# Gate and up projections: the order of rounded-weight and residue matmuls, two contraction tiles at a time

## What is computed

```python
def swiglu(h, w_gate, w_up, w_down):
    return (jax.nn.silu(h @ w_gate) * (h @ w_up)) @ w_down

x = x + swiglu(rms_norm(x, ffn_norm[i]), w_gate[i], w_up[i], w_down[i])
```

## Time and profile before

| | before |
|---|---|
| median of 3 runs | 1276.21 us (1276.15 to 1276.36) |
| span of the profiled execution | 1274.6 us |
| instructions | 17805 |
| matmuls | 7056, and as many weight loads |
| granted TensorE clock, mean | 0.999 |
| DMA, mean over the span | 176 GB/s |

### The profile page before, as it was taken

How to read it: one execution, slowest core, us unless ns; L and a number is a source line. 1 busy time by engine, 2 the same in 40 slices (tenths; PEclk the granted TensorE clock), 3 DMA queues, 4 the chain that set the end, 5 groups by cost and what they waited for, 6 DMA issues and landing times.

```text
span 1274.6 us, 17805 instructions
## 1 busy us (share of the span) xinstructions
PE 1263.7 (99%) x7056; PEld 1088.4 (85%) x7056; DVE 904.9 (71%) x1283; ACT 717.6 (56%) x1059; POOL 104.9 (8%) x137
## 2 busy tenths in 40 slices
PE   9999999999999999999999999999999999999997
PEld 8998778888888888888888888888888998888886
DVE  6967665776676685776666857777667897766665
ACT  5865454655555684654445545555555865654543
POOL 2000000000000440000000000000000781000000
PEclk9999999999999999999999999999999999999999
DMA  8443236465663312355554643686654523455551
GB/s 293 166 165 133 99 103 225 139 230 212 223 229 123 138 65 102 133 203 193 199 198 165 211 162 132 237 300 226 213 212 170 193 111 132 170 203 203 193 177 62
DMA packets 32802, 224.42 MB, mean 176 GB/s; under 512 B 3776, under 2 KB 4160, under 8 KB 7248
## 3 DMA queue, kind: packets, MB, share of 16 engines
q1 hardware_dynamic: 32576, 223.22, 49.3%
q10 hardware_dynamic: 144, 0.07, 0.0%
HBM read 222.23 MB, written 1.05 MB: 175 GB/s over the span
## 4 chain that ended last, share of the span: by engine, by line
PE 98%; DVE 1%; DMA 0%; ACT 0%; issue 0%; POOL 0%; ACTq 0%; SPq 0%; DVEq 0%; POOLq 0%
PE pb L496 25%; PE pb L467 16%; PE pb L469 16%; PE pb L468 16%; PE pb L498 13%; PE pb L473 3%; PE pb L1049 2%; PE pb L563 1%; PE pb L860 1%; PE pb L884 1%; PE pb L565 1%; PE pb L624 1%; PE pb L636 1%; PE pb L1108 0%; DMA xt<-d_x 0%; PE pb L691 0%
## 5 line engine op out<-in xcount | busy, mean ns | idle before, releaser
L1678 DVE TENSOR_TENSOR wlo<-raw,whi 128x2048 fp32r<-128x2048 f32 (+2 forms) x194 | 428.0, 2207 | 188.1 <-ACT whi L1162 187.7
L496 PE MATMUL pb<-both,whi 128*128 128x512 f32 x1344 | 476.0, 398 | 0.0
L1162 ACT ACTIVATE whi<-raw 128x2048 fp32r<-128x2048 f32 (+1 forms) x196 | 372.0, 1900 | 66.1 <-PE pb L469 59.6
L498 PE MATMUL pb<-both,wlo 128*128 128x256 f32 x1344 | 377.2, 281 | 0.0
L496 PEld LDWEIGHTS pb<-both,whi 128*128 128x128 f32 x1344 | 252.4, 188 | 61.5
L467 PE MATMUL pb<-whi,both 128*128 128x512 f32 (+2 forms) x728 | 286.3, 393 | 0.0
L469 PE MATMUL pb<-whi,both 128*128 128x512 f32 (+2 forms) x728 | 282.0, 387 | 0.0
L468 PE MATMUL pb<-wlo,both 128*128 128x512 f32 (+2 forms) x728 | 281.4, 386 | 0.0
L498 PEld LDWEIGHTS pb<-both,wlo 128*128 128x128 f32 x1344 | 253.8, 189 | 1.5
L1165 ACT ACTIVATE arena<-pb 128x256 f32<-128x256 f32 (+1 forms) x234 | 94.9, 418 | 243.4 <-PE pb L498 159.6
L469 PEld LDWEIGHTS pb<-whi,both 128*128 128x128 f32 x728 | 136.6, 188 | 28.8
(11 more groups left out here) (159 smaller groups left out, 1192.5 us busy)
## 6 DMA issues: line engine op xcount, KB each, us to landing
raw<-d_ws SPq DMA_DIRECT2D x198, 1024.0 KB, 4.9
raw<-d_ws SPq DMA_DIRECT2D x5, 768.0 KB, 4.3
arena<-d_diag SPq DMA_DIRECT2D x4, 960.0 KB, 7.8
raw<-d_ws SPq DMA_DIRECT2D x2, 576.0 KB, 3.6
arena<-d_c SPq DMA_DIRECT2D x1, 1060.0 KB, 4.8
xt<-d_x SPq DMA_DIRECT2D x2, 512.0 KB, 4.6
raw<-d_ws SPq DMA_DIRECT2D x2, 512.0 KB, 7.2
arena<-d_rows SPq DMA_DIRECT2D x2, 512.0 KB, 6.0
```

The lines of the kernel that those rows point to most:

```text
L496: e.matmul(b[:, :], wh[:, k, fs], both[:, k, :], start=k == 0, stop=k == 7, skip_group_check=True)
L498: m = e.matmul(b[:, 256:512], wl[:, k, fs], ahi[:, k, :], start=False, stop=k == 7, skip_group_check=True)
L1162: e.activation(split_parts(n)[0], raw_part(n), ACT.Copy).then_inc(*sig("act.hi", f"hi{n}"))
L1678: e.tensor_tensor(l[:, a:b], raw_part(n)[:, a:b], f32(h[:, a:b]), ALU.subtract).then_inc(*sig("dve.lo", f"lo{n}"))
```

## The change

In `paired` the loop over the eight tiles k becomes a loop over four pairs of tiles. For each pair the two matmuls of L496 (rounded weights, 512 columns) are issued first, for k0 and k0 + 1, and then the two of L498 (residues, 256 columns). The first and the last matmul of a block, the flags that start and end the accumulation, the banks, the signals and every other function stay as they are. The additions into a bank's second half come in another order.

```diff
--- before.py
+++ after.py
@@ -491,12 +491,14 @@
                     if mid and i == 1:
                         mid()
                     b = claim(names[i], spot + i)
-                    for k in range(8):
-                        fs = slice(128 * i, 128 * i + 128)
-                        e.matmul(b[:, :], wh[:, k, fs], both[:, k, :], start=k == 0, stop=k == 7,
-                                 skip_group_check=True)
-                        m = e.matmul(b[:, 256:512], wl[:, k, fs], ahi[:, k, :], start=False, stop=k == 7,
+                    fs = slice(128 * i, 128 * i + 128)
+                    for k0 in range(0, 8, 2):
+                        for k in (k0, k0 + 1):
+                            e.matmul(b[:, :], wh[:, k, fs], both[:, k, :], start=k == 0, stop=k == 7,
                                      skip_group_check=True)
+                        for k in (k0, k0 + 1):
+                            m = e.matmul(b[:, 256:512], wl[:, k, fs], ahi[:, k, :], start=False, stop=k == 7,
+                                         skip_group_check=True)
                     m.then_inc(*sig(key, f"{done}.{i}", *([f"done{n}"] if i else [])))
 
             def moving(key, n, bs, ncols, k0, done=None, first=None, mid=None, at_k=2):
```

## The result

| | before | after |
|---|---|---|
| median | 1276.18 us (1276.09 to 1276.36, 4 runs) | 1268.77 us (1268.63 to 1268.83, 4 runs) |
| ratio | | 0.9941, 95% interval 0.9927 to 0.9955 |
| span of the profiled execution | 1274.6 us | 1267.0 us |
| granted TensorE clock, mean | 0.999 | 0.999 |

The changed kernel is 7.4 us faster. First its page: the span, the busy times and the chain that ended last by engine.

A forecast was written before the change was run, and what follows sets the result against it. TensorE was taken as the bound, through distances between matmul starts. Terms of -4.1 us and +0.5 us, with down chunks at zero, gave -3.6 us: span 1271.0 us, median 1272.6 us, range 1268.0 to 1281.5 us.

The forecast's parts named there:

- What bounds it: Whole kernel: TensorE busy 99%, no wait in gate or up matmuls, so time is the sum of distances between matmul starts.
- The sign and the range: Whole kernel: faster by 3.6 us, with a range from 1268.0 to 1281.5 us.
- settled-rhythm rival: Gate and up groups fall into a settled rhythm at 692.8 ns, -8.2 us, total 1268.0 us; chance 0.12.
- The group term: Gate and up: 592 groups in the usual state go from 706.6 to 699.7 ns, -4.1 us.
- the even split: Gate and up: the extra 6.9 ns a pair goes half to each of two changes of width.
- The second reading: Gate and up group worked out from neighbouring matmuls: 0.46 + 0.117 + 0.12 = 0.70 us.
- The quick blocks: Gate and up: 80 groups already quick at 693.2 ns may lose 6.5 ns each, +0.5 us.
- The down chunks: Entries into 40 down chunks, first ten wide matmuls 2.33 us instead of 2.26: put at zero, 2.8 us either way.
- Unsettled wides: Gate and up: two wide matmuls behind a narrow one stay at 0.48 us, +7.8 us, 1284.0 us; chance 0.22.
- Order costs nothing: Gate and up: no price for order, or the same; group 706.6 ns everywhere, +1.1 us, 1277.3 us; chance 0.24.
- The form of it in which a load doesn't fit: Gate and up: the 6.9 ns come from a weight load not fitting under a narrow matmul, so nothing is gained.

The follow-up runs named there:

- g4: Kernel before, with `paired` issuing four 512-column matmuls, then four 256-column ones, twice a block; 1272.74 us, ratio 0.9973.
- g8: Kernel before, with `paired` issuing all eight 512-column matmuls of a block, then the eight 256-column ones; 1270.08 us, ratio 0.9952.
- abba: Kernel before, with every two tiles in `paired` issued wide, narrow, narrow, wide, so a block ends with a wide matmul; 1268.90 us, ratio 0.9943.
- lastgroup: Kernel before, old order except the last two tiles of each up chunk, issued wide, wide, narrow, narrow; 1275.12 us, ratio 0.9991.
- entry: Kernel before, old order except the first two tiles of each gate chunk, issued wide, wide, narrow, narrow; 1274.77 us, ratio 0.9989.
- dummy: Kernel before, old order, with one small 32-column fp32 matmul added ahead of each gate chunk behind a down chunk and of gate 1; 1277.17 us, ratio 1.0008.
- alt320: Kernel before, old order, with the narrow matmul widened from 256 to 320 columns; 1311.42 us, ratio 1.0276.

## Why the prediction was right, point by point

- **What bounds it** held: PE alone, no wait on the changed lines, weights in time; the time followed the distances between starts to the last microsecond.
- **The sign and the range** held (1268.0 to 1281.5). The time, 1268.8 us, lies nearer to the settled-rhythm rival (1268.0) than to the forecast (1272.6), so the size was too small by half: -7.4 us against -3.6.
- **The group term** was mis-sized. I charged 6.9 / 2 ns for each change of width and got 699.7 ns; measured 696.7. What failed is the even split, a constant price for each change of width: g4 and g8 show that there is none, and that of the run lengths tried two, four and eight, two is the cheapest. The second reading, 0.46 + 0.117 + 0.12, is 0.697 before I rounded it to 0.70. It meets the measured mean, but by parts that were wrong both ways: 0.466 for the wide two and 0.230 for the narrow two. That the sum had the right sign was owed in part to luck: by the same reasoning g4 should have been faster still, and it is 4 us slower.
- **The quick blocks** did get worse as expected: 693.3 to 696.7 a group, 3.4 ns where I had charged 6.5. Of the 148 blocks in the usual state, the 36 right behind a down chunk win 33 ns each (2810 to 2777) and the 112 others 40 (2827 to 2787), together -5.7; with +0.3 for the quick ones gate and up give -5.4 where -3.6 was forecast.
- **The down chunks** are the term put at zero with 2.8 us either way: 36 of the 40 entries fell from 2.330 to 2.277 us and four from 2.309, together -2.0 us. abba, lastgroup and entry show that it hangs on the state in which the stream before arrives, which both the last group and a group 30 pairs earlier can move. This term is half of what was missing.
- **Unsettled wides**, the rival on the other side, had a true mechanism with the wrong case: 0.48 us for two wide ones is what the first pair of a down chunk takes behind the old order. Inside the new groups two wide ones take 0.463 to 0.469 us (233 + 230 and 233 + 236 by turns, by the starts), 0.466 in the mean; only right behind a down chunk they take 0.453. The forecast let 0.473 decide the sign; by its own terms the total is even at a group of 705 ns, so at 0.468, and the measured mean lies only just under it. In g4 and g8, with more wide ones in a run, more of the settling is paid.
- **Order costs nothing**, with the Trainium skill's N/2.4 + 2.5 ns (TensorE: Matmul & The Clock Gate, Back-to-back issue gap; the section gives it as the gap of an isolated matmul, which the forecast left out) behind it, is excluded. The pure streams here take 226.7 and 120.0 ns in place of its 215.8 and 109.2, and order counts: g4, g8 and the changed kernel run the same matmuls at 2807, 2793 and 2787 ns a block, and dummy runs one order at two speeds. The form of it in which a load doesn't fit fell with alt320, as far as the estimate of the pure 320-column stream holds.
- **Settled rhythm** was the closest in total and right in kind: two groups repeat every 1.393 us. It was wrong in that the pattern is not free; it costs 3.3 ns a group over the pure streams.

## What to carry to other kernels

Where TensorE is the bound and has no waits, read the distances between the starts of matmuls, not their durations, and compare each mixed stream with the pure ones: 2% of a stage can lie in the order of widths alone. The best order is not the one with the fewest changes of width, so try several run lengths (one, two, four and all, here), and look at the untouched stream behind as well, since a quarter of this gain fell there. A stream that runs at two speeds in one trace shows that order and entry have a price there.

## What the hardware showed that was not expected

One stream of the same fp32r matmuls, with the clock granted in full and no wait, has two steady speeds, 346.7 and 353.3 ns for a wide and narrow pair, and keeps the one that it was entered with until the widths change. The quick speed comes in two forms: pairs of 347 ns throughout in the kernel before, pairs of 350 and 343 by turns in dummy. All the steady patterns return to a step of 6.67 ns: a wide matmul of the pure stream takes 226.7 ns (34 steps), a narrow one 120.0 (18), three pairs 1040 (156) or 1060 (159), the pair with 320 columns 380 (57), two groups of the changed kernel 1393 (209), a block of g8 2793 (419) and of g4 2807 (421). The single distances inside a pattern do not keep to it (361 and 349 ns, for example); their sum over a period does. The step is sixteen periods of the 2.4 GHz clock that is granted here. Matmuls that have to meet a slot of this length, with the distance of one deciding the place of the next in it, would look like this; that is argued from the numbers and not shown. Which unit sets the step, and why a small fp32 matmul mostly finds the quick pattern where other orders do not, stays open. So does whether the width itself is what counts: in every version a narrow matmul adds to one part of the bank that wide ones write whole, and no run separates the two.
